# First chunk of two squared-ReLU MLPs by quarter products, and sums over features with two columns at their end

## The reference, cut to what matters

```python
def squared_relu_mlp(h, w1, w2):
    return jnp.square(jax.nn.relu(h @ w1)) @ w2        # w1 1024 x 4096, w2 4096 x 1024

def rms_norm(x, g):
    xf = x.astype(jnp.float32)
    y = xf * lax.rsqrt(jnp.mean(xf * xf, axis=-1, keepdims=True) + NORM_EPS)
    return (y * g.astype(jnp.float32)).astype(x.dtype)

h = modulate(rms_norm(x, mlp_norm[layer]), sh_m, sc_m)   # h * (1 + scale) + shift
x = x + gt_m * squared_relu_mlp(h, mlp_w1[layer], mlp_w2[layer])
```

## Time and profile before

| what | us |
|---|---|
| median of 3 runs | 2426.03 (2424.86 to 2428.92) |
| the profiled execution, its time | 2426.29 |
| the profiled execution, its span | 2424.5 |
| PE busy | 2290.5 (94%) |
| DVE busy | 1206.0 (50%) |
| ACT busy | 509.0 (21%) |
| mean granted clock of PE | 0.972 |

### The profile page before, as it was taken

The page is one execution under the profiler, slowest core; times in us unless marked ns, Lnnn a source line. Parts: engine busy times, 40 slices in busy tenths (PEclk is TensorE's granted clock), DMA queues, the critical chain, the costliest instruction groups (busy, mean ns, idle before and its releaser), DMA issues. The chain is left out here.

```text
span 2424.5 us, 26465 instructions
## 1 busy us (share of the span) xinstructions
PE 2290.5 (94%) x9806; PEld 1522.8 (63%) x9806; DVE 1206.0 (50%) x2762; ACT 509.0 (21%) x1149; POOL 43.0 (2%) x50
## 2 busy tenths in 40 slices
PE   7999899999999999989999999999999998889886
PEld 4444586888887655558688888844578443333332
DVE  4444575667776256666455666567566111111014
ACT  2233212330002144441233100112232000000001
POOL 0000000000000000000000000000000000000000
PEclk9999999999999999999999999899998999999999
DMA  7544313353532211103444444311033679999995
GB/s 298 222 161 175 116 70 138 140 208 139 208 140 113 70 53 53 61 35 139 180 167 181 166 181 167 139 70 70 1 139 141 227 328 427 426 427 426 423 424 220
DMA packets 45459, 452.73 MB, mean 187 GB/s; under 512 B 7784, under 2 KB 7784, under 8 KB 20240
## 3 DMA queue, kind: packets, MB, share of 16 engines
q1 hardware_dynamic: 37616, 435.64, 45.0%
q0 software_dynamic: 6528, 12.17, 1.4%
q10 hardware_dynamic: 1184, 3.19, 0.3%
HBM read 444.54 MB, written 18.39 MB: 191 GB/s over the span
## 5 line engine op out<-in xcount | busy, mean ns | idle before, releaser
L2996 PE MATMUL ps<-ring,big 128*64 128x512 f32 (+1 forms) x768 | 233.5, 611 | 28.1 <-issue 15.9
L1193 PE MATMUL ps<-big,ring 128*128 128x256 f32 x768 | 185.8, 379 | 0.6 <-PE ps L1111 0.6
L2996 PEld LDWEIGHTS ps<-ring,big 128*64 128x64 f32 (+1 forms) x768 | 85.4, 151 | 146.9 <-issue 133.8
L3092 DVE TENSOR_TENSOR big<-big,ps 128x512 f32<-128x512 f32 x20 | 13.8, 688 | 295.5 <-ACT big L3061 281.4
L537 PE MATMUL ps<-hT,ring 128*128 128x512 f32 x336 | 153.7, 607 | 5.9 <-DMA ring<-in_stream 5.9
L1193 PEld LDWEIGHTS ps<-big,ring 128*128 128x128 f32 x768 | 145.8, 190 | 21.1 <-issue 1.4
L1111 PE MATMUL ps<-hT,ring 128*128 128x256 f32 x672 | 154.3, 379 | 1.5 <-ACT big L1260 1.5
L2077 PE MATMUL ps<-hT,ring 128*128 128x512 f32 x320 | 144.1, 606 | 2.8 <-DVE big L2459 1.7
L1111 PEld LDWEIGHTS ps<-hT,ring 128*128 128x128 f32 x672 | 127.5, 190 | 20.3 <-issue 3.1
L1025 DVE SCALAR_TENSOR_TENSOR ring<-ring,tmp 128x1024 f32<-128x1024 f32 x112 | 136.1, 1219 | 0.0
L2996 PE MATMUL ps<-big 128*64 128x512 f32 (+1 forms) x352 | 128.9, 600 | 7.1 <-ACT big L3057 3.3
(11 more groups left out here) (509 smaller groups left out, 3664.2 us busy)
## 6 DMA issues: line engine op xcount, KB each, us to landing
ring<-in_stream SPq DMA_DIRECT2D x99, 2048.0 KB, 8.5
ring<-in_gate SPq DMA_DIRECT2D x17, 2048.0 KB, 29.7
ring<-in_up SPq DMA_DIRECT2D x16, 2048.0 KB, 25.8
ring<-in_down SPq DMA_DIRECT2D x15, 2048.0 KB, 28.6
big<-in_up SPq DMA_DIRECT2D x9, 2048.0 KB, 25.5
big<-in_down SPq DMA_DIRECT2D x8, 2048.0 KB, 27.6
big<-in_gate SPq DMA_DIRECT2D x7, 2048.0 KB, 24.3
hT<-in_down SPq DMA_DIRECT2D x5, 2048.0 KB, 27.1
```

Source lines behind the costliest of these rows:

```text
L1193: ins = pe.matmul(m.ps[:, bank[name], q * H:(q + 1) * H], a[:, q * P:(q + 1) * P], b, start=(first and q == 0), stop=(final and q == 1))
L2996: ins = pe.matmul(out[a:z, :], left[:, k * P + a:k * P + z], bufs[i % WBUF][:, k * width + c * 512:k * width + (c + 1) * 512], start=(k == ...
L3092: dve.tensor_tensor(hid[:, s, :], hid[:, s, :], m.ps[:, 3 + 2 * s, :], ALU.mult).then_inc(hid_ok, 1)
```

## The change

`pairs` now has all 8 chunks, 16 pairs. The plain products of the first chunk and their ReLU and square are gone. P1 and P2 of the first two pairs are issued first, each of their steps waiting for its tile of h; P1 and P2 of the second pair go to bank 7, after `scale_rows` has read it (`scaled_ok`). The rest of pairs 0 and 1 follows (P6, P5, P7, P4, P3 each), then pairs 2 to 15 as before. DVE's order at the beginning is t1, t2, the first three weight sums, t3, t4, the fourth weight sum; the conditioning rows of the first chunk are done in the loop, one after c11 and one after the fourth weight sum, as for every chunk. At the end, the sums of the accumulators stand after step 24 of the 32 steps of w2, and every sum has two columns: (1, squared gain of the tile) in the second MLP, where the weighted squares of the last four tiles are no longer made.

```diff
@@ phase_mlp
-    pairs = [(c, q) for c in range(1, 8) for q in range(2)]
+    pairs = [(c, q) for c in range(8) for q in range(2)]
+    def position(i, name):
+        if i < 2 and name in ("P1", "P2"):
+            return 2 * i + int(name[1])
+        if i < 2:
+            return 4 + 5 * i + ("P6", "P5", "P7", "P4", "P3").index(name) + 1
+        return PRODUCTS * i + ("P1", "P6", "P5", "P7", "P2", "P4", "P3").index(name) + 1
+    def place(i, name):
+        if i == 1 and name in ("P1", "P2"):
+            return m.ps[:, 7, H * (name == "P2"):H * (name == "P2") + H]
+        return m.ps[:, bank[name], 0:H]
-    inner2 = m.tmp[:, 1024:1032]
+    factors = m.tmp[:, 1024:1040].rearrange("p (f c) -> p f c", c=2)
+    either = m.tmp[:, 1040:1044].rearrange("p (f c) -> p f c", c=2)
+    sums_at = m.ps[:, 7, 0:2 * NT].rearrange("p (i c) -> p c i", c=2)
@@ PE
-                def product(name, a, b):
-                    out = m.ps[:, bank[name], 0:H]
+                def product(i, name, a, b, k0=None):
                     for k in range(4):
-                        ins = pe.matmul(out, a[:, k, :], b[:, k, :], start=(k == 0), stop=(k == 3))
+                        if k0 is not None:
+                            pe.wait_ge(h_ok, k0 + k + 1)
+                        ins = pe.matmul(place(i, name), a[:, k, :], b[:, k, :], start=(k == 0), stop=(k == 3))
                     ins.then_inc(prod, 1)
...
-                w = chunk.rearrange("p (k n) -> p k n", k=8)
-                for j in range(4):
-                    for k in range(KT):
-                        if j == 0:
-                            pe.wait_ge(h_ok, k + 1)
-                        last = pe.matmul(m.ps[:, j, :], w[:, k, j * P:(j + 1) * P], m.hT[:, k, :],
-                                         start=(k == 0), stop=(k == KT - 1))
-                    last.then_inc(mm, 1)
-                pe.wait_ge(mm, 4)
-                pe.sem_inc(m.free[at % RING], 1)
-                pe.wait_ge(t_ok, 1)
-                pe.wait_ge(relu, 4)
-                pe.wait_ge(cond_ok, 1)
+                pe.wait_ge(m.full[chunk1(0)[0]], chunk1(0)[1])
+                for i in range(2):
+                    a11, a12, a21, a22 = quarters(*pairs[i])
+                    if i:
+                        pe.wait_ge(scaled_ok, 1)
+                    product(i, "P1", a11, b11, 0)
+                    product(i, "P2", a12, b21, 4)
                 for i, (c, q) in enumerate(pairs):
...
-                    product("P1", a11, b11)
+                    if i > 1:
+                        pe.wait_ge(p1_ok, i)
+                        product(i, "P1", a11, b11)
...
+                    pe.wait_ge(t_ok, 1)
                     pe.wait_ge(s12_ok, i + 1)
...
+                    pe.wait_ge(cond_ok, 1)
+                    pe.wait_ge(t_ok, 2)
+                    product(i, "P4", a22, t4)
...
+                def token_sums(sq, factor, start, stop):
+                    for i in range(NT):
+                        ins = pe.matmul(m.ps[:, 7, 2 * i:2 * i + 2], sq[:, i * P:(i + 1) * P], factor,
+                                        start=(start and i == 0), stop=(stop and i == NT - 1))
+                    return ins
...
                     products(s, ["P6", "P5", "P7", "P2", "P4", "P3"])
+                    if s == 24:
+                        pe.wait_ge(freed, 3)
+                        if inner is None:
+                            token_sums(sq1.acc, m.ones[:, 0:2], True, False)
+                        else:
+                            pe.wait_ge(freed2, 3)
+                            pe.wait_ge(weighed, 1)
+                            token_sums(sq1.acc, either[:, 0, :], True, False)
+                            token_sums(sq2.acc, either[:, 1, :], False, False)
...
-                keep_busy(m, pe, 7, 4)
+                pe.wait_ge(v1_ok, 2)
+                keep_busy(m, pe, 0, 4)
                 for j in range(4, 8):
                     pe.wait_ge(sqd, j + 1)
-                    token_sums(m.ps[:, 1, 0:NT], sq1.at(j), False, j == 7).then_inc(summed, 1)
-                    if inner is not None:
-                        pe.wait_ge(sqd2, j + 1)
-                        token_sums(m.ps[:, 2, 0:NT], sq2.at(j), False, j == 7).then_inc(summed2, 1)
-                keep_busy(m, pe, 7, 3)
+                    token_sums(sq1.at(j), m.ones[:, 0:2] if inner is None else factors[:, order[j], :], False, j == 7
+                               ).then_inc(summed, 1)
+                keep_busy(m, pe, 0, 3)
@@ ACT
-                for j in range(4):
-                    act.wait_ge(mm, j + 1)
-                    act.activation(hid[:, j, :], m.ps[:, j, :], ACT.Relu).then_inc(relu, 1)
-                    act.wait_ge(relu, j + 1)
-                    act.activation(hid[:, j, :], hid[:, j, :], ACT.Square).then_inc(squared_ok, 1)
...
-                        if inner is not None and j < 6:
+                        if inner is not None and j < 4:
                             square_rows(m, act, sq2, inner, j, freed2, sqd2, order[j])
@@ DVE
                 scale_rows(m, dve, outs, hs)
+                dve.wait_ge(hs, KT)
+                dve.sem_inc(scaled_ok, 1)
                 dve.wait_ge(h_ok, KT)
                 c1.link(dve.tensor_tensor(t1, b12, b11, ALU.subtract))
-                c1.link(dve.tensor_tensor(t2, b22, t1, ALU.subtract))
+                dve.tensor_tensor(t2, b22, t1, ALU.subtract).then_inc(t_ok, 1)
+                sums_a(*pairs[0])
+                dve.tensor_tensor(b12, b22, b12, ALU.subtract).then_inc(t3_ok, 1)
+                dve.wait_ge(t_ok, 1)
                 dve.tensor_tensor(t4, b21, t2, ALU.subtract).then_inc(t_ok, 1)
-                sums_a(*pairs[0])
                 sums_b(*pairs[0], 0)
                 dve.wait_ge(cond_ok, 1)
-                ada(0, 0, 4)
-                dve.wait_ge(mm, 4)
-                dve.wait_ge(t_ok, 1)
-                dve.tensor_tensor(b12, b22, b12, ALU.subtract).then_inc(t3_ok, 1)
...
-                    c2.link(dve.tensor_tensor(inner2, inner, inner, ALU.mult))
+                    c2.link(dve.memset(factors[:, :, 0], 1.0))
+                    c2.link(dve.memset(either, 0.0))
+                    for j in range(2):
+                        c2.link(dve.memset(either[:, j, j:j + 1], 1.0))
+                    dve.tensor_tensor(factors[:, :, 1], inner, inner, ALU.mult).then_inc(weighed, 1)
...
-                if inner is not None:
-                    for j in (6, 7):
-                        f = order[j]
-                        dve.wait_ge(summed2, j - 5)
-                        dve.scalar_tensor_tensor(sq2.at(j), m.xT[:, f, :], inner2[:, f:f + 1], m.xT[:, f, :], ALU.mult, ALU.mult
-                                                 ).then_inc(sqd2, 1)
...
-                    dve.wait_ge(summed2, 4)
-                    c2.link(dve.tensor_scalar(m.st[:, 0:NT], m.ps[:, 1, 0:NT], EPS, None, ALU.mult))
-                    dve.tensor_tensor(m.st[:, 0:NT], m.st[:, 0:NT], m.ps[:, 2, 0:NT], ALU.add).then_inc(whole, 1)
+                    c2.link(dve.tensor_copy(m.st[:, NT:2 * NT], sums_at[:, 0, :]))
+                    dve.scalar_tensor_tensor(m.st[:, 0:NT], m.st[:, NT:2 * NT], EPS, sums_at[:, 1, :], ALU.mult, ALU.add
+                                             ).then_inc(whole, 1)
```

More of the change, by code:

```diff
@@ L1069, in squares_of @@
     def squares_of(c):
-        return 4 + 8 * (2 * c + 1)
+        return 16 * (c + 1)
     with Phase(nc) as ph:
         sem = ph.sem
-        mm, relu, cond_in, cond_ok, mod_done, chn, zeroed, hs, h_ok = (sem(s) for s in (
-            "mm", "relu", "cond_in", "cond_ok", "mod_done", "chn", "zeroed", "hs", "h_ok"))
+        cond_in, cond_ok, mod_done, chn, zeroed, hs, h_ok = (sem(s) for s in (
+            "cond_in", "cond_ok", "mod_done", "chn", "zeroed", "hs", "h_ok"))
         prod, t_ok, t3_ok, s12_ok, s3_ok, s4_ok, p1_ok, u2_ok, u3_ok, u4_ok, c11, c12, c21, c22, flat = (sem(s) for s in (
@@ L1080, in phase_mlp @@
             "c22", "flat"))
-        squared_ok = sem("squared_ok")
+        squared_ok, scaled_ok = sem("squared_ok"), sem("scaled_ok")
         added, mod2_done, chn2, sqd, freed, sqd2, freed2, summed, whole, rooted, inverse = (
@@ L1145, in _ @@
                         pe.wait_ge(u2_ok, i)
-                    product("P6", s2, t2)
+                    product(i, "P6", s2, t2)
                     if i:
@@ L1149, in _ @@
                         pe.wait_ge(c22, i)
-                    product("P5", s1, t1)
+                    product(i, "P5", s1, t1)
                     if i:
@@ L1220, in _ @@
                         products(s, [name])
-                def token_sums(out, sq, start, stop):
-                    for i in range(NT):
-                        ins = pe.matmul(out[:, i:i + 1], sq[:, i * P:(i + 1) * P], m.ones[:, 0:1],
-                                        start=(start and i == 0), stop=(stop and i == NT - 1))
-                    return ins
-                pe.wait_ge(v4_ok, 2)
```

(19 more changed lines are left out.)

38 lines of the change are left out of this document (15 added, 23 removed).

## The result

The changed kernel takes 2407.65 us (median of 4 runs, 2407.09 to 2409.76); the kernel before, run beside it, 2425.45 (4 runs). The ratio is 0.9929 (95% interval 0.9913 to 0.9945). Over all runs of the two kernels in this study before's mean is 2426.0 (58 runs) and after's 2408.5 (14 runs): 17.5 us less, where 13.0 were forecast. One more run of before took 4797.09 us, nearly twice the rest, and is left out here and in every ratio.

A forecast was written before the change was run, and what follows sets the result against it. PE was taken as the bound, busy 94% of the span. Gains of 6.46 us (beginnings), 0 (first end) and 6.5 (second end) sum to 13.0: 2426.03 - 13.0 = 2413.1 us, range 2408.8 to 2417.5.

The forecast's parts named there:

- The beginnings: Start of each MLP: products replace the first chunk's plain matmuls, gaining 3.39 and 3.07 us, together 6.46.
- thin margin at P6: Beginning, pair 0: P6's DVE sum ready at 367.25, PE arrives at 367.33; cost taken as 0, margin 0.08 us.
- rival 1: Beginnings: DVE eats the gain, 1 us or more lost in each MLP; 2415 to 2418 us, chance 0.10.
- rivals 4 and 5: New beginnings: clock falls to 0.50 (2461 us), or weight loads emerge from under shorter matmuls (2455); together chance 0.02.
- the first end: End of the first MLP, including moved sums: change 0, bounds -2.3 to +1.0 us.
- The moved sums: Accumulators' sums, moved into w2's streams, still cost 0.99 us in the first MLP and 1.89 in the second.
- The four fills: Small DVE fills before w2's first sums, second MLP only: cost 0, bounds 0 to 0.8 us.
- The second end: End of the second MLP: 32 of 64 sums and a DVE wait go, gaining 6.5 us (5.4 to 8.4).
- D + 4.4: Second MLP's end: the clock falls 4.4 us after the products end, making the moved sums plus end 11.7 us.
- rival 3: Both ends: the clock stays up, gaining 17.2 us in all; 2408.9 us, chance 0.07.
- the chains of 7.5 and 8.0 us: Ends at full clock: 5.2 us to sums done, then 2.3 in the first; next phase after 8.0 in the second.
- Nothing behind gives it back: Later phases: PE waits for no transfer in traced stretches, later loads move along, so none of the 13.0 us is lost.

The follow-up runs named there:

- e9: The changed kernel, unchanged, run for a third profile; 2410.67 us, ratio 0.9930 to the kernel before.
- e7: The changed kernel with the 32 sums at the second MLP's end made twice, the second time into another bank; 2414.06 us, ratio 0.9956.
- e11: The changed kernel with one 128x512 all-ones matmul per tile for the sums at the first MLP's end, no spread; 2415.07 us, ratio 0.9954.
- e1: The changed kernel with only the new beginnings of both MLPs and the old ends; 2418.93 us, ratio 0.9968.
- e5: The changed kernel with one product (P7 of the second MLP's ninth pair) computed twice; 2409.05 us, ratio 0.9926.
- e6: The changed kernel with one product (P7 of the second MLP's ninth pair) computed three times; 2413.80 us, ratio 0.9944.
- e3: The kernel before, unchanged, run for a second profile; 2427.44 us, ratio 1.0002.
- e4: The changed kernel, unchanged, run for a second profile; 2407.07 us, ratio 0.9923.
- e8: The changed kernel with the accumulators' sums moved from w2's stream back behind the last product; 2411.82 us, ratio 0.9936.
- e12: The changed kernel with 128x512 sums at the first MLP's end and the last slot's release moved behind `keep_busy`; 2412.09 us, ratio 0.9949.

## Why the prediction was right or wrong

**The beginnings: right.** Forecast 3.39 and 3.07 us, measured 3.35 and 3.02 (200.44 to 197.09, 200.12 to 197.10). P6 of pair 0 came at 8.3 us, just outside the 7.7 to 8.2 named, pair 2's P1 at 25.48 for 25.0 to 25.5; DVE was busy 21.93 of 25.48 us, and no wait of PE for it stands in the trace behind the thin margin at P6. That speaks against rival 1; the clock of 1.00 and 25.48 us for the whole chunk exclude rivals 4 and 5.

**The streams and the first end: right.** The moved sums cost 0.89 and 1.78 us in the streams (0.99 and 1.89 forecast). With them the first end's net is -0.83 + 0.89 = +0.06, for a forecast of 0. The four fills cost nothing that shows.

**The second end: right in kind, the size off.** Net -9.59 + 1.78 = -7.8 us, for -6.5 (a gain of 5.4 to 8.4 in the bounds). The forecast let the clock fall at D + 4.4; here it fell at D + 6.6 (1546.8, D being the end of the products), which is half way to rival 3, and in e9 earlier, with 6.4 us at half clock and an end of 10.12. Take half of the low time off, and the new ends are 7.0 (first: 10.02 - 3.05; e9 9.70 - 2.75) and 6.9 to 7.6 us (second: 10.12 - 3.2, 8.70 - 1.1): the chains of 7.5 and 8.0 us that the forecast built were 0.4 to 1.1 us too long.

**The step that failed** is "Nothing behind gives it back", with the later phases unchanged and their clock at 0 in the sum and in the range. The measured 2407.65 us are 5.45 below the forecast 2413.1. In profiles the six places gave 14.1 us (13.0 in e9), at most 1.1 more than the sum and that from the second end, well within the 8.7 to 17.5 of the bounds. The rest of the span is not a constant. Its code is the same in the five profiles of the table, and it took 1604.1 and 1600.6 us in before, 1599.3, 1600.9 and 1603.9 in after; over all 14 profiles of the study it goes from 1595.1 (e7) to 1609.8 (e11). The two stretches right behind the MLPs follow the clock: less half their time at 0.50, they are 373.4 (before), 373.8 (after), 372.1 (e9) and 372.3 (e1) us, and 275.4 (before), 275.5 (again), 275.0 (after) and 274.8 (e9); over all 14 profiles 372.1 to 373.8 and 273.9 to 275.5. So of the 18.9 us between the two first profiles 14.1 are the change, 3.35 are 6.7 us less at half clock behind the second MLP, and the remaining 1.4 is the sum of small differences ahead, between and in the last, DMA-heavy phase, whose length (574.0 to 579.2 over the profiles) followed nothing that was found. Against before's second profile after's span is 15.4 us shorter, and 14.1 of it are the six places: most of the excess is gone with another execution of the old kernel.

**The range was also added up wrongly.** The bounds of the terms are 4.5 and 8.5 for the beginnings, -0.8 and 0 for the fills, -1.0 and 2.3 for the first end, 5.4 and 8.4 for the second. Together they give 8.1 to 19.2 us, and not 8.7 to 17.5. The upper one would have put the range's lower edge at 2406.8, below the measured 2407.65. That would have been luck: it would have let the ends pay for what the later phases did.

The Trainium skill's page "TensorE: Matmul & The Clock Gate" (What's actually happening) says that the check on activity is not tied to the kernel's start. The prediction applied that to the two ends only. The runs of one unchanged kernel agree with it beyond them: same code, 385.7 or 389.1 us between the MLPs.

**What stays open.** The means differ by 17.5 us, the places by 13.0 to 14.1 in after's profiles, and by 16.0 and 14.9 in e5 and e6 less their repeated products. The 1.5 to 4.5 between them is less than the 4.6 by which the untouched part differs among after's own three profiles, so it can be the luck of the executions. It can also be that the changed kernel meets the good pattern more often, for a reason in its code; two profiles of before and three of after don't decide it. The single times lean that way. Before's 58 times leave a gap between 2423.25 and 2424.55, with 11 below it (mean 2422.5; e3's profile is one) and 47 above (2426.8). After's 14 are less clear: 8 lie from 2405.07 to 2407.92 (mean 2406.6), 6 are spread from 2409.00 to 2413.12 (2411.1). Lower against lower the change is worth 15.9 us, upper against upper 15.7, and the rest of the 17.5 would be that after lands in the lower group more often. But this split was made after the fact, e4's profile has the shorter stretches behind both MLPs and is in the upper group (2409.00), and nothing here shows a cause in the code: e5 and e6, which moved the work behind by 1.7 and 3.5 us, gave none.

## What to carry to other kernels

Forecast an edit by the places it touches, but where PE is the bound and its clock comes and goes, give every long stretch that is not edited a term of its own in the range. Here the untouched part differed by 3.5 us between two profiles of one kernel, by 4.6 among three of the other, and by 14.7 over all 14. When two profiles are compared, take half of the time at the low clock off each long stretch in which PE is the bound: behind the MLPs that brought the untouched stretches together to 1.7 us. It did not hold ahead of the first MLP, where after's first two profiles have 17.1 and 44.4 us at half clock and are 356.9 and 357.5 us long. Add up the bounds of the terms once more before the range is written down. And when a stage's end is a row of tiny matmuls, their count is the price, so one matmul with two columns for two with one is a real saving.

## What the runs showed of the hardware

- A matmul with two columns costs what one with one costs: 16 sums take 1.97 us in either form (and e8).
- The clock of unchanged code comes in a few patterns: 23.3 to 23.9 or 33.8 to 34.9 us at half clock in the 385 to 390 us between the MLPs (14 profiles), and in one and the same kernel 10.7 or 17.2 in the 280 to 283 behind the second, where all profiles together go from 6.3 to 21.3.
- With 128x512 matmuls in the first MLP's end the clock stayed at 1.00 where with rows of 128x1 or 128x2 it did not (e11, e12: 0.1 us of the end at half clock or less, in the twelve other profiles 1.7 to 6.8). Two profiles show it; that the wide matmuls are the cause is likely and not shown.
- The reciprocal on DVE takes 3.36 us for 128x512, 6.6 ns a column, about five times a subtraction of that shape. The Trainium skill's page "VectorE: DVE Perf Modes" (First, the fixed hardware budget) has it as an iterative divide; a time well above a subtraction's agrees with that, and no run here shows more of it.
